# A decoder layer on one core: rows of x turned by products with a diagonal matrix of 1/rms

## The reference, cut to what matters

```
def rms_norm(x, g):
    xf = x.astype(jnp.float32)
    y = xf * lax.rsqrt(jnp.mean(xf * xf, axis=-1, keepdims=True) + RMS_EPS)
    return (y * g).astype(x.dtype)
...
    h = rms_norm(x, norm_mix[l])
    proj = h @ w_in[l]
    u_pool, u_rwkv, u_nsa = split_cols(proj, [POOL_COLS, RWKV_COLS, NSA_COLS])
...
    x = x + merged @ w_out[l]
    h = rms_norm(x, norm_ffn[l])
    x = x + hier_moe(h, w_router_grp[l], b_router_grp[l], w_router_exp[l], b_router_exp[l],
                     w_exp_gate[l], w_exp_up[l], w_exp_down[l])
return rms_norm(x, norm_final)
```

## Time and profile before

| what | value |
|---|---|
| median of 3 runs | 640.22 us (640.09 to 640.49) |
| the profiled execution's own time | 640.59 us |
| its span, first to last instruction | 638.8 us |
| TensorE busy | 596.5 us, 93% |
| VectorE, ScalarE, GpSimd busy | 216.1, 142.7, 19.9 us |
| mean granted TensorE clock | 0.977 |
| DMA | 158.95 MB, mean 249 GB/s |

### The profile page before, as it was taken

The page is one execution under the profiler, slowest core; times in us unless marked ns, Lnnn a source line. Parts: engine busy times, 40 slices in busy tenths (PEclk is TensorE's granted clock), DMA queues, the critical chain, the costliest instruction groups (busy, mean ns, idle before and its releaser), DMA issues.

```text
span 638.8 us, 11809 instructions
## 1 busy us (share of the span) xinstructions
PE 596.5 (93%) x4968; PEld 432.8 (68%) x4968; DVE 216.1 (34%) x586; ACT 142.7 (22%) x366; POOL 19.9 (3%) x23
## 2 busy tenths in 40 slices
PE   8999999999999999999999999998988988958694
PEld 7988887878877877778888888884434533414331
DVE  3152448625334766356220322233111111101022
ACT  3110234042234453444330000001110111000023
POOL 1000000000200103001000000000000000000000
PEclk9999999999999999999999999998999989969798
DMA  8584344841211121102336997978999999999993
GB/s 326 196 324 171 124 145 158 316 139 67 88 47 69 68 68 68 68 27 107 122 97 261 422 421 280 425 315 313 424 419 419 422 420 421 420 421 421 422 390 123
DMA packets 27416, 158.95 MB, mean 249 GB/s; under 512 B 3025, under 2 KB 7265, under 8 KB 9569
## 3 DMA queue, kind: packets, MB, share of 16 engines
q1 hardware_dynamic: 24352, 137.71, 55.1%
q10 hardware_dynamic: 3008, 20.45, 7.7%
HBM read 157.07 MB, written 1.07 MB: 248 GB/s over the span
## 4 chain that ended last, share of the span: by engine, by line
PE 61%; issue 22%; DMA 7%; SPq 4%; DVE 3%; ACT 2%; POOL 0%; POOLq 0%; DVEq 0%; ACTq 0%
PE bank L620 27%; PE bank L1235 7%; DMA ring<-experts 6%; PE bank L1299 4%; SPq L583 4%; PE bank L1244 4%; PE bank L1308 3%; PE bank L846 3%; PE bank L652 2%; PE bank L955 2%; PE bank L984 2%; PE bank L1004 1%; DVE work L1810 1%; PE bank L968 1%; DMA table<-params 1%
## 5 line engine op out<-in xcount | busy, mean ns | idle before, releaser
L620 PE MATMUL bank<-hT,ring 128*128 128x256 f32 x864 | 199.4, 383 | 0.4 <-ACTq L1447 0.3
L620 PEld LDWEIGHTS bank<-hT,ring 128*128 128x128 f32 x864 | 159.6, 190 | 30.4 <-issue 10.6
L620 PE MATMUL bank<-yT,ring 128*128 128x256 f32 x256 | 55.4, 379 | 0.0
L620 PEld LDWEIGHTS bank<-yT,ring 128*128 128x128 f32 x256 | 48.6, 190 | 6.6
L1810 DVE TENSOR_TENSOR work<-bank,table 128x512 f32<-128x512 f32 (+1 forms) x22 | 11.6, 544 | 97.2 <-PE bank L1244 90.5
L1299 PE MATMUL bank<-ring,work 128*32 128x512 f32 (+1 forms) x192 | 36.0, 667 | 7.8 <-DMA yT<-experts 6.6
L1244 PEld LDWEIGHTS bank<-work,tok 128*128 128x128 f32 x256 | 31.0, 196 | 10.2 <-issue 10.2
L1435 ACT ACTIVATE work<-bank 128x512 f32<-128x512 f32 (+2 forms) x45 | 23.4, 519 | 55.1 <-PE bank L1299 42.5
L1244 PE MATMUL bank<-work,tok 128*128 128x128 f32 x256 | 32.5, 282 | 0.5 <-DVEq L2319 0.5
L1308 PE MATMUL bank<-work 128*128 128x512 f32 (+1 forms) x68 | 30.4, 584 | 1.3 <-ACT work L1435 0.7
L1609 ACT ACTIVATE tok<-tok,small 128x128 f32<-128x128 f32 (+1 forms) x64 | 28.5, 445 | 12.5 <-DVE small L2038 10.5
(11 more groups left out here) (258 smaller groups left out, 720.3 us busy)
## 6 DMA issues: line engine op xcount, KB each, us to landing
ring<-front SPq DMA_DIRECT2D x47, 1024.0 KB, 5.0
ring<-experts SPq DMA_DIRECT2D x40, 1024.0 KB, 24.3
work<-experts SPq DMA_DIRECT2D x9, 1024.0 KB, 27.6
ring<-experts ACTq DMA_DIRECT2D x8, 1024.0 KB, 14.8
table<-experts SPq DMA_DIRECT2D x6, 1024.0 KB, 26.9
yT<-experts SPq DMA_DIRECT2D x6, 1024.0 KB, 26.8
hT<-experts SPq DMA_DIRECT2D x4, 1024.0 KB, 24.6
work<-experts ACTq DMA_DIRECT2D x3, 1024.0 KB, 27.8
```

The costliest lines, as they stand in the source:

```text
L620: return first(pe.matmul(o, l, r, start=(k == 0), stop=(k == n - 1)))
```

## The change

The rows are no longer normalised before they are turned. VectorE multiplies the 128x128 identity by the roots (one per partition), which gives a diagonal matrix `rootdiag` for each row tile, and TensorE multiplies the raw block of `tok` by it. The block is the stationary operand, so the result is the block turned and each of its columns (a row of x) scaled by its root. `rootdiag` lies where the first of the 8 column tiles of `xn` lay. Both banks of a row tile now wait for one count of `xn_ready`, and the wait for the constants stands before `normalise` on VectorE.

```
-        xn = mix[:, 0:8, :].rearrange("p c t -> p (c t)").rearrange("p (i d) -> p i d", i=2)
+        rootdiag = mix[:, 0, :].rearrange("p (i t) -> p i t", i=2)
...
             def turn_rows(i):
 
+                pe.wait_ge(q[f"x_loaded{i}"], 16)
+                pe.wait_ge(q["xn_ready"], i + 1)
                 for n in (2 * i, 2 * i + 1):
-                    pe.wait_ge(q["xn_ready"], n + 1)
-                    if n == 0:
-                        pe.wait_ge(q["lead_loaded"], 32)
                     o = begin(f"xT{n}")
                     for k in range(4):
                         kk = (n % 2) * 4 + k
-                        last = pe.transpose(o[:, k * P:(k + 1) * P], xn[:, i, kk * P:(kk + 1) * P], ident)
+                        last = pe.matmul(o[:, k * P:(k + 1) * P], tok[:, i, kk * P:(kk + 1) * P], rootdiag[:, i, :],
+                                         start=True, stop=True)
                     end(last, f"xT{n}")
...
             def normalise(i):
 
+                dve.wait_ge(q["lead_loaded"], 32)
                 dve.wait_ge(q["root_ready"], i + 1)
-                for n in range(2):
-                    part = slice(512 * n, 512 * (n + 1))
-                    chain(ts(xn[:, i, part], tok[:, i, part], stat[:, 8 + i:9 + i], None, ALU.mult), "xn_ready", hold=False)
+                chain(ts(rootdiag[:, i, :], ident, stat[:, 8 + i:9 + i], None, ALU.mult), "xn_ready", hold=False)
...
-            dve.wait_ge(q["lead_loaded"], 32)
             to_hT(1)
```

## The result

| | changed kernel | kernel before | ratio, 95% interval |
|---|---|---|---|
| 22 and 22 executions | 641.24 us median (640.43 to 643.4) | 640.38 us median (639.55 to 641.59) | 1.0016 (1.0008 to 1.0023) |

The change costs 0.86 us in the medians (0.13%) and 1.02 us in the means (0.16%, the ratio of the table; its interval is 0.5 to 1.5 us), where 1.47 us was forecast. The kernel is slower, as forecast, but by less than 0.2%; the forecast had given a little over one half to a cost above that line.

What follows compares the result with a forecast made beforehand. TensorE, busy nine tenths or more for some 440 us, was taken to bound the front part; first turn 0.57 plus second turn 0.90 gave +1.47 on 640.22, so 641.7 us, with 8 in 10 between 640.6 and 642.5.

Steps and rivals of the forecast that it cites:

- Price of a product: On TensorE, a turned block leaves two records instead of one and costs 0.222 us where it cost 0.109.
- Rival A: At the turns, products are as cheap as transposes, leaving only the earlier start: -0.20 us, 640.0; chance 0.04.
- VectorE's operation: At the start, one 128x128 multiply takes 0.28 us, so the diagonal is ready 0.20 us earlier than the first piece was.
- First turn: Row tile 0: VectorE's second-bank copy ends last, so the first projection product starts at 9.65, not 9.08: +0.57 us.
- Cover of the second diagonal: Before the second turn: diagonal ready at 11.68, TensorE reaches it at 12.3; 0.6 us of cover, so no cost.
- Second turn: Row tile 1, on TensorE alone: eight products instead of eight transposes add 0.90 us; the copies are covered.
- Late zeros: At the start, the forecast had the products of zeros end at 6.60, leaving room for the first product at 6.72.
- theory C: Experiments' theory: the whole delay is there at the start, but a share of about 0.4 is swallowed later.
- all behind it is TensorE's chain, which shifts: After the two turns, the whole +1.47 us is handed on through TensorE and the expert loads to the end.
- Its own bounds for the shift: Whole kernel: +1.0 to +1.9 us, from the bounds of the start and the runs' 0.4 us spread.
- Rival C: Behind the router, TensorE's clock dip moves or vanishes, first slot back 1.34 us sooner: +0.1, 640.4; chance 0.08.

Runs made afterwards that it cites:

- five products at the router: Five unread products instead of two while TensorE waits for the router: kernel before 640.05 us (1.0004), changed kernel 640.85 us (1.0009), both against 639.92 us.
- the three sets: The changed kernel with no further edit, measured three times against the kernel before: 641.24 us (1.0016), 641.75 us (1.0024), 641.13 us (1.0013).
- third run: The changed kernel with no further edit, measured a third time against the kernel before: 641.13 us against 640.19, ratio 1.0013 (1.0002 to 1.0025).
- the 9 products: Kernel before with 9 products of zeros (2.00 us of work) added behind the second turn: 642.85 us against 640.19, ratio 1.0042.
- 15 products of zeros: Kernel before with 15 products of zeros (3.33 us of work) added behind the second turn: 642.48 us against 640.19, ratio 1.0036.

## Why the prediction was right, step by step

The forecast reads an execution whose zeros ended early, so such an execution is the fair one to hold against its steps. It is the changed kernel with five products at the router (640.15 us), whose start has no other edit. The chain of waits, start and length:

```profile
6.47 0.30 DVE work L1814
6.76 0.14 issue
6.90 2.04 PE bank L645 x16
8.94 0.02 issue
8.96 0.70 DVE hT L1810
9.66 0.09 issue
9.75 2.85 PE bank L652 x24
12.60 1.79 PE bank L645 x16
```

- *Price of a product.* Right: L645 has 32 records on TensorE, and eight products take 1.79 us at the second turn, so 0.224 us each. Rival A falls.
- *VectorE's operation.* Right: 0.29 us against 0.28.
- *First turn.* Right in size and in who ends last. Line by line it is 0.1 to 0.2 us late: the root came 0.09 later and the hand-over of the diagonal took 0.14 us, not 0.04. The first projection product comes at 9.75 against 9.65, +0.67 to the earlier trace rows.
- *Cover of the second diagonal.* Right: in this execution VectorE made it at 11.70 to 11.98, and TensorE came to it at 12.60.
- *Second turn.* Right: +0.92 against +0.90.
- *Late zeros.* Missed. The products of zeros end anywhere from 6.36 to 7.67 us. Where they end late they hold back either kernel's first turn, and what VectorE saves buys nothing: L698 is at 26.67 in the changed kernel and 25.02 in the kernel before, both with zeros of 5.9 us, +1.65. With early zeros it is 26.08 against 24.50, +1.58.

So by the trace the start is some 1.6 us later, slightly more than the 1.47 forecast. Yet the three sets measured 0.86 to 1.39 us. Where the rest went was theory C's question, and a place that can take a part of it was found. At 39 us TensorE takes the first chunk that SP refilled. SP issues that refill behind the load of the bias table. The DMA issues of that load, in the kernel before, in its copy with five products, in the changed kernel and in its third run (KB each, us to landing):

```profile
ring<-bias_rows SPq DMA_DIRECT2D x1, 2048.0 KB, 9.1
```

```profile
ring<-bias_rows SPq DMA_DIRECT2D x1, 2048.0 KB, 9.6
```

```profile
ring<-bias_rows SPq DMA_DIRECT2D x1, 2048.0 KB, 8.1
```

```profile
ring<-bias_rows SPq DMA_DIRECT2D x1, 2048.0 KB, 7.9
```

In the profiles with the slow load TensorE's weight loads stand still for the refill. The weight loads of the kernel before with five products, and of the changed kernel, at that place:

```profile
39.65 1.38 PEld L620 LDWEIGHTS bank<-hT,ring 128*128 128x128 f32 x7 [0.68 <-DMA ring<-front]
```

```profile
39.82 2.35 PEld L620 LDWEIGHTS bank<-hT,ring 128*128 128x128 f32 x11
```

All four profiles that start as the kernel before does (its own two, and the two with five products at the router) have this wait, 0.2 to 0.7 us; none of the four of the changed kernel has it. Only the longer waits reach the router. From L698 to L1205 the kernel before took 408.8 and 408.7 us in its own two profiles, with a wait of 0.2 us in each, as the changed kernel did in its four (408.6 to 408.7). The two copies with five products, with waits of 0.7 and 0.4 us, took 409.5 and 409.0. So the step "all behind it is TensorE's chain, which shifts" holds nearly whole between the kernels as they are: with L698 later by 1.69 us (26.45 against 24.76, means of three and two profiles) the router is later by 1.66. With the copies counted, four profiles each, L698 is later by 1.71 us (26.36 against 24.64) and the router by 1.39 (435.04 against 433.65), so that some 0.3 us are given back at 39 us. How often the kernel before has the long wait these profiles do not show.

The same place bears on the 9 products that cost no less than their 2.0 us. In their profile SP's store of 24 KB, on whose landing the load of the bias table waits, took 3.4 us in place of the 1.5 of every other profile, the refill came later by as much, and TensorE's weight loads stood still for 1.17 us:

```profile
bias_rows<-work SPq DMA_DIRECT2D x1, 24.0 KB, 3.4
```

```profile
42.22 0.94 PEld L620 LDWEIGHTS bank<-hT,ring 128*128 128x128 f32 x5 [1.17 <-DMA ring<-front]
```

The router is 2.66 us late there, against the mean of 433.65. That execution took 641.87 us and lies in the quicker of the two groups, so the wait does not explain the groups. Whether other executions with 9 products have it is not known.

A shift of 1.4 us at the router lies inside all three intervals of the changed kernel's time (0.5 to 1.5, 0.9 to 2.2 and 0.1 to 1.6 us), and the forecast's 1.47 at the edge of the first. One of 1.66 lies above two of them. The distance with five products on both sides, at most 1.0 us, fits neither. The wait at 39 us is a candidate there: in this pair's profiles the router of the changed kernel is only 0.62 us later (434.65 against 434.03), as the kernel before had its longest wait in that one. Whether it is so in the other executions was not shown, and the cause of what is missing in the times stays open. The error of such a comparison is not small beside it: the repeated kernel before came out 0.33 us off in the medians, and the two groups of executions move a median by which of them holds the middle. Whether the fall comes more often in one kernel than in the other was not settled. That 15 products of zeros cost less than their 3.3 us, beyond the interval, while 9 cost no less than their 2.0, suggests that it also matters where a delay puts the router; these runs do not show how.

So the steps at the start are right in mechanism and size; the cost in the times is below the forecast, and the range covered that. Its own bounds for the shift, +1.0 to +1.9 us, hold the three means but not two of the three medians. The forecast also started from the median of three executions, 640.22, which was 0.16 us below that of 22, and this brought its 641.7 nearer to the result. Rival C was given 0.08 on the ground that the fall came every time. That ground was wrong, though the forecast did not suffer. The chances have a slip of 0.01: their parts make 0.39 for no change that can be told and 0.02 for faster, where 0.38 and 0.03 stand.

## What to carry to other kernels

A float32 transpose left one record here and a product two at the same pace, so turning by a diagonal matrix doubled TensorE's share; it can pay only where the multiply that it saves is on the path and TensorE is not. Here VectorE saved 0.2 us on the path and TensorE paid 1.8 (16 more records), 1.6 us net. Where two engines hand over nearly level, ask which of them a longer step reaches last: the second bank waits for all eight products. And three executions within 0.1% do not prove that a clock stretch seen in one profile comes every time: look at a second profile of the same kernel first.

## What the runs showed of the hardware

- TensorE started its products of zeros at 1.75 us in each profile. 26 records took from 4.61 to 5.92 us: the slowest is a pace of 0.22 us a record to the end (5.65 us over 25), and the quickest is 0.17 in the mean (4.34 over 25), where later products run at 0.11. The profile's granted clock reads 1.00 over all of them in every profile, so the rows do not show that a low clock is the reason. A longer start need not be the edit's doing.
- At the router the granted clock falls to 1.2 GHz in some executions of one kernel and not in others (four of the ten profiles without extra products at the router), and what lies behind the router is then 1.7 us longer in the mean. In three profiles with a rest of 1.39 us filled it did not fall.
- The 2 MB load of the bias table took 9.1 to 9.6 us in six profiles and 7.9 to 8.7 in seven. In the six it was issued 4.6 to 6.2 us after the last of the first loads had landed, in the seven 6.5 us or more. No experiment tried the cause.
